# The down product of each expert step moved in front of the next step's up product, in one layer with 64 routed experts

## What is computed

```python
def swiglu(x, wg, wu, wd):
    return (jax.nn.silu(x @ wg) * (x @ wu)) @ wd
...
    idx, wts = route(h2, w_router[i], router_bias[i])
    moe = routed_experts(h2, idx, wts, w_exp_gate[i], w_exp_up[i], w_exp_down[i]) \
        + swiglu(h2, w_sh_gate[i], w_sh_up[i], w_sh_down[i])
    x = x + moe.reshape(B, S, D)
```

## Time and profile before

| | us |
|---|---|
| median of 3 runs | 1059.02 |
| lowest and highest run | 1058.03, 1060.67 |
| profiled execution: span from first to last instruction | 1058.3 |
| of it TensorE matmuls busy | 963.5 |
| VectorE, ScalarE, GpSimd busy | 288.1, 161.2, 168.7 |

### The profile page before, as it was taken

How to read it: one execution, slowest core, us unless ns; L and a number is a source line. 1 busy time by engine, 2 the same in 40 slices (tenths; PEclk the granted TensorE clock), 3 DMA queues, 4 the chain that set the end, 5 groups by cost and what they waited for, 6 DMA issues and landing times.

```text
span 1058.3 us, 15067 instructions
## 1 busy us (share of the span) xinstructions
PE 963.5 (91%) x6147; PEld 433.8 (41%) x6147; DVE 288.1 (27%) x652; ACT 161.2 (15%) x293; POOL 168.7 (16%) x320
## 2 busy tenths in 40 slices
PE   5999999999999899999999999999988887882598
PEld 4554554444444343343333333333323222330487
DVE  3322641002212562344322111111101010110982
ACT  2002230150000101111111111211111111210111
POOL 3235000000001011222222222222221212101100
PEclk9999999999999899999999999999989998996699
DMA  9351211121231818999999999999999999988931
GB/s 334 126 159 42 78 40 53 68 79 40 87 143 36 361 53 325 379 401 407 416 408 413 417 408 405 397 406 373 421 422 421 420 422 421 417 368 306 402 157 40
DMA packets 70692, 292.87 MB, mean 277 GB/s; under 512 B 8204, under 2 KB 30240, under 8 KB 43616
## 3 DMA queue, kind: packets, MB, share of 16 engines
q1 hardware_dynamic: 57872, 255.96, 61.1%
q0 software_dynamic: 12176, 33.86, 8.3%
q10 hardware_dynamic: 576, 2.10, 0.5%
HBM read 275.63 MB, written 25.69 MB: 285 GB/s over the span
## 4 chain that ended last, share of the span: by engine, by line
PE 72%; DMA 22%; DVE 3%; SPq 1%; issue 1%; ACT 1%; POOL 0%; POOLq 0%; DVEq 0%
PE ps L1705 21%; DMA ring<-in_w_exp_up 19%; PE ps L1433 11%; PE ps L1733 8%; PE ps L1813 5%; PE ps L1535 5%; PE ps L1417 3%; PE ps L1377 3%; PE ps L1520 3%; PE ps L1518 3%; PE ps L1354 3%; DMA ring<-accumulator 2%; PE ps L1581 2%; PE ps L1383 1%; PE ps L1566 1%
## 5 line engine op out<-in xcount | busy, mean ns | idle before, releaser
L1705 PE MATMUL ps<-ring,gates 128*32 128x512 f32 x2624 | 298.5, 608 | 34.0 <-DMA ring<-in_w_exp_up 32.5
L1705 PEld LDWEIGHTS ps<-ring,gates 128*32 128x32 f32 x2624 | 91.4, 112 | 235.1 <-issue 233.3
L1733 PE MATMUL ps<-ring,poolbuf 128*32 128x512 f32 x1312 | 149.3, 595 | 1.7 <-ACT actT L768 0.9
L1204 DVE COPY poolbuf<-ps 128x256 f32<-128x256 f32 x41 | 17.4, 425 | 412.8 <-PE ps L1716 412.8
L1433 PE MATMUL ps<-actT,ring 128*128 128x512 f32 x256 | 112.3, 595 | 0.0
L597 POOL TENSOR_TENSOR tickets<-cst 128x1 f32<-128x1 f32 x79 | 14.9, 189 | 393.6 <-ACT actT L768 387.9
L1733 PEld LDWEIGHTS ps<-ring,poolbuf 128*32 128x32 f32 x1312 | 38.8, 109 | 88.7 <-issue 87.4
L1433 PEld LDWEIGHTS ps<-actT,ring 128*128 128x128 f32 x256 | 47.9, 190 | 59.6 <-issue 59.5
L768 ACT ACTIVATE actT<-ps,qT 128x1024 f32<-128x1024 f32 x41 | 45.7, 1114 | 149.2 <-PE ps L1733 149.2
L1354 PE MATMUL ps<-cst,rows 128*128 128x128 f32 x392 | 53.1, 281 | 13.0 <-DMA cst<-in_constants 10.2
L558 POOL TENSOR_SCALAR st<-st 128x1 f32<-128x1 f32 (+2 forms) x17 | 7.4, 434 | 337.2 <-ACT rows L730 241.9
(11 more groups left out here) (226 smaller groups left out, 849.4 us busy)
## 6 DMA issues: line engine op xcount, KB each, us to landing
ring<-in_w_exp_gate SPq DMA_DIRECT2D x64, 1024.0 KB
ring<-in_w_exp_up SPq DMA_DIRECT2D x64, 1024.0 KB, 18.6
ring<-in_w_exp_down SPq DMA_DIRECT2D x64, 1024.0 KB, 14.7
ring<-accumulator SPq DMA_DIRECT2D x16, 1024.0 KB, 11.9
ring<-in_w_gate SPq DMA_DIRECT2D x8, 1024.0 KB, 13.1
ring<-in_w_in SPq DMA_DIRECT2D x5, 1024.0 KB
ring<-in_w_out SPq DMA_DIRECT2D x4, 1024.0 KB
ring<-in_w_ple_gate SPq DMA_DIRECT2D x4, 1024.0 KB
```

The source lines that it names most:

```text
L1705: last = mm(bank(2 + k)[part, :], hgT[k][:, q, part], pair_view(EXPERT_SLOT[js[c]])[:, q], start=(q == 0), stop=(q == KD - 1))
L1733: last = mm(bank(6 + half)[part, :], eactT[r % 2][:, q, part], w[:, q, half * 512:(half + 1) * 512], start=(q == 0), stop=(q == 1))
```

## The change

In step r TensorE now does `up(r)`, `rows_T(r + 1)`, `acts_T(r)`, the lists or the shared part, `down(r)`. Before, `acts_T` and `down` of step r - 1 stood in step r. VectorE copies the transposed activation of step r at the end of its part of step r, behind the copy of the next rows. ScalarE weighs step r in step r, but step 0 in step 1, since its weights are there only then. The order of SyncE's loads and of GpSimd's gathers and scatters is not edited. The whole diff:

```diff
--- before.py
+++ after.py
@@ -787,9 +787,10 @@
                     rows_hi(r + 1, (r + 1) % 2)
                 if JOB_AT + 2 * NT <= r < JOB_AT + JOBS:
                     ple_square(r - JOB_AT - 2 * NT)
+                if r == 1:
+                    weigh(0)
                 if r:
-                    weigh(r - 1)
-            weigh(STEPS - 1)
+                    weigh(r)
 
             def o_start(j):
                 all_scattered(act)
@@ -1219,11 +1220,10 @@
                                         gpost[:, half * 512:(half + 1) * 512], ALU.mult).then_inc(ple_copied, 1)
 
             for r in range(STEPS):
-                if r:
-                    act_T(r - 1, (r - 1) % 2)
                 act_rows(r, r % 2)
                 if r + 1 < STEPS:
                     rows_T(r + 1, (r + 1) % 2)
+                act_T(r, r % 2)
                 if 1 <= r < NGROUP:
                     dve.wait_ge(list_ps, r + 1)
                     rows_of(r, found_of(r))
@@ -1237,7 +1237,6 @@
                     base(n)
                 elif 2 * NT <= n < JOBS:
                     ple_gain(n - 2 * NT)
-            act_T(STEPS - 1, (STEPS - 1) % 2)
 
 
             nc.vector.tensor_copy(o_iota, cst[:, C_IOTA:C_IOTA + CAP]).then_inc(o_iota_ready, 1)
@@ -1738,10 +1737,9 @@
             rows_T(0)
             for r in range(STEPS):
                 up(r)
-                if r:
-                    acts_T(r - 1)
                 if r + 1 < STEPS:
                     rows_T(r + 1)
+                acts_T(r)
                 if 1 <= r < NGROUP:
                     lists(r)
                 n = r - JOB_AT
@@ -1749,10 +1747,7 @@
                     shared_down(n)
                 elif 2 * NT <= n < JOBS:
                     ple_proj(n - 2 * NT)
-                if r:
-                    down(r - 1)
-            acts_T(STEPS - 1)
-            down(STEPS - 1)
+                down(r)
 
 
             def o_start(j):
```

## The result

| | before | after |
|---|---|---|
| median of 4 runs on the same chip, us | 1059.85 (1058.03 to 1061.28) | 1120.26 (1118.25 to 1124.62) |
| profiled span, us | 1058.3 | 1118.1 |

The ratio is 1.056 (95%: 1.0528 to 1.0591). The change costs 60 us; I had forecast 50 of them. In the profiled execution the span grew by 59.8 us.

The account below looks back on a forecast made before the run. TensorE and DMA were taken to bound in turn, both busy from 450 to 600 us, DMA full from 850. 7.1 + 37.6 + 4.4 - 4 + 5 = 50.1 us gave 1109 us, range 1087 to 1126.

Parts of the forecast that it names:

- Part 2: Start: step 1's down product newly waits for the weighing of step 0, which needs the list weights; +7.1 us.
- Part 1: Every step: TensorE waits for its own step's activation before the down product; a list step grows from 12.34 to 12.71 us.
- Part 3: Three-step groups: the first down product waits some 3.3 us for a matrix loaded fifth in its burst; +37.6 us.
- Part 6: Clock: waits in three-step groups drop TensorE to 1.2 GHz, at five of eleven, 1.5 us each; +5 us, bounds 0 and +14.
- Part 4: Second half, two-step groups: DMA engines stay full, 17.4 us a batch against 12.8 us of waiting and products; costs nothing.
- Part 5: End: step 39's down product, ahead of step 40's up product, waits for queued matrices, +4.4 us; earlier final weights, -4.
- rival 4: Three-step groups: the clock falls in every group, up and down products slow, +14 instead of +5 us; 1125 us, chance 0.14.
- Rival 1: Three-step groups: the fifth load lands early enough, only a group's own length counts; 1077 us, chance 0.10.
- Rival 2: Faster: earlier down-matrix loads fill the DMA gap at 700 to 725 us, and the end only gains; 1050 us, chance 0.03.
- Rival 3: Whole kernel: no change, the faster case's gain and the start's 7.1 us cancel; 1059 us, chance 0.03.

Follow-up runs that it names:

- the kernel with the fifth load moved: Changed kernel, with the second expert's down matrix in three-step groups loaded ahead of gate and up of the third and fourth experts: 1083.23 us, ratio 1.0207.
- all loads matched: Changed kernel, with all SyncE expert loads in the new order of use, down matrices ahead of the next gate and up matrices: 1073.94 us, ratio 1.0113.
- transposes in front: Changed kernel, with 24 unread transposes on TensorE in front of the down products of steps 1, 3, 6 and so on to 24: 1115.69 us, ratio 1.0531.
- the second half alone: Kernel before, with the new product order in steps 27 to 40 only and the loads as before: 1063.43 us, ratio 1.0028.
- half of the fifth load's bytes: Changed kernel, loading only the first half of the second expert's down matrix in groups 1 to 9: 1112.6 us, ratio 1.0513.
- the new order in the first half only: Kernel before, with the new product order in steps 0 to 26 only and the loads as before: 1121.03 us, ratio 1.0545.
- the end alone changed: Kernel before, with the new order for steps 39 and 40 only, step 39's down matrices loaded ahead of step 40's up matrices: 1059.76 us, ratio 0.9994.

## Why the prediction was right, and where it was off

The sum in four stretches, in profiled spans; the forecast for the groups includes the clock's 5.

| | forecast | measured |
|---|---|---|
| start, up to U(2) (part 2) | +7.1 | +9.4 (427.23 - 417.88) |
| U(2) to U(26) (parts 1, 3, 6) | +42.6 | +49.6 (773.05 - 427.23 = 345.8 for 296.2) |
| U(26) to the end of D(40) (parts 4, 5) | +4.4 | +6.4 (252.4 for 246.0) |
| behind D(40) (part 5) | -4 | -5.6 (92.7 for 98.3) |
| sum | +50.1 | +59.8 |

U(0), in front of the change, starts 0.6 earlier than before (395.55 for 396.13), so the start costs 9.9 counted from there.

**Part 1, right.** Where no load is late, D starts 2.3 us behind its up product, and seven of the eight groups of the kernel with the fifth load moved last 38.2 to 38.6 us; 3 x 12.71 is 38.1. Over U(2) to U(26) the steps' own lengthening is 12.0 us there (308.2 for 296.2), where 8 x 38.1 and the shared product's 1 give 9.8. With all loads matched it is the larger of the two costs left.

**Part 2, right in its wait, short by the clock.** D(1) starts at 420.73 (forecast 421.45) after 3.08 us for the weighing. But it then takes 6.50 us, and I had summed 3.57. With transposes in front, 3.64 and U(2) at 424.0. These 2.9 us more are what the start has over the 7.1, counted from U(0). I had put the clock's loss at the groups only and forgotten that this new wait is as long as theirs.

**Part 3, right.** The start of D(3k) was taken at 18.3 + 0.14 behind the up product's end; measured are 17.0 to 19.6, on average 18.0. To a tenth all but the 19.6 lie between my bounds (17.0 and 19.3). D(3k) waits in every group. What I had cited against it (the Trainium skill, "DMA: Bandwidth & Descriptors", section "Where 436 GB/s comes from": 435 GB/s, by which there would be no wait) the traces don't bear out for a burst like this one. The kernel with the fifth load moved shows that this one load's place is worth 37 us. That is not the +37.6 of my sum, though the numbers are alike: mine held the steps' own lengthening (9.8) and no slow product, the measured one is the wait (23.4) and the slow products (14.4). For the wait alone I had 37.6 - 9.8 = 27.8. The rate between 430 and 750 us is 346 GB/s, not my 380.

**Part 4, right in its price, a little over its own bound.** From the start of U(28) to that of U(38) a group of two steps lasts 34.5 to 35.3 us, 35.0 on average. That is over the 34.7 at which I wanted to call myself wrong. Before, from U(30) on, where its loads set the pace, such a group lasted 34.6 to 34.8. So the sign has come, by some 0.3 us a group. The bound was drawn too close for the claim that it was to test: from U(26) to U(40) the kernel takes 8.7 us more (237.8 for 229.2), just what part 5 has up to that point (5.0 + 0.14 + 3.57), the DMA share from 850 to 900 us is 1.01 (before 1.02), and the second half alone costs 3 us. The wait of D stands once in each group, before D(28), D(30) and so on to D(38), 3.7 to 5.4 us (besides 0.5 and 1.0 before D(33) and D(35)), and not before nearly every D, as I had written.

**Part 5, right in both signs, but D(39) didn't wait as I had it.** The chain at the end of the kernel after:

```profile
1007.31 3.57 PE ps L1732 x32
1010.88 6.99 PE ps L1704 x64
...
1020.01 5.43 PE ps L1732 x32
...
1034.15 14.68 DMA ring<-accumulator
```

D(39), U(40) and D(40) follow one another as I had them, with a slow D(40), 1.8 too long: this is most of the 2.0 us over the forecast. But the 5.0 us for two queued down matrices were not what set D(39). They landed at 1006.2, and D(39) started at 1007.24 with no idle time in front. What it followed was TensorE's own path: D(38), which waited 3.7 us for its matrices and then took 6.57, the up product of step 39, and 3.2 us of transposes and per-layer product. The two paths end within 1.1 us of each other, so that the number of this step came out is partly luck. Behind D(40) it gained 5.6 where I took 4, inside the bounds: 3.6 up to the start of the accumulator's read (8.7 us for 12.3), 3.3 in the read, and 1.3 were lost again behind it.

**Part 6, the term that was mis-sized.** I took the share of slow products from the kernel before, five of eleven, and 1.5 us each: +5. Seven of eight were slow, by 1.3 to 2.9 us: +14.4, as sums of what they took over 3.64. That is what rival 4 said, and of its 14 us it was nearly exact, though it had U slow as well, and no U was. The rule behind that rival (the Trainium skill, "TensorE: Matmul & The Clock Gate", section "HAM oscillation — how this bites in real kernels": the wait for data at every tile re-throttles the engine at every tile) agrees with seven of eight. I should have weighed it more: in the kernel before, the slow products all lay where DMA hid them, and their rate there said little about a wait of another length. Yet rival 4's sum was too simple as well, and so was my own: both add the slow product to the group's length in full. The run with the transposes took 11.4 us of slow products away and got 4.3 back. The sum of part 3 and part 6 is near the measured one (-0.4 x 8 = -3.2 for the earlier landing, +14.4 for the slow products, less the 5 that I had taken: 6.2 of the 7.0 us missing), but this is bookkeeping along TensorE's path. It is not what each cause is worth if removed: a slow D and the wait in front of it are exchanged for one another through the loads.

**Rival 1** (the loads hide it) came true only when the order of the loads was mended: its 1077 stands beside 1083 (the fifth load moved) and 1074 (all matched). Its 15 us for 24 steps don't follow from the 38.1 for 36.9 us beside them, which give 9.6. **Rival 2** needed the down matrices of step 39 ahead of the up matrices of step 40; given just that, with D(39) moved too, the time did not change (0.9994). D(39) was indeed done ahead, but U(40) started 8.5 later with the two matrices ahead of its own. **Rival 3** was not seen.

**What stays open.** What decides whether a given product runs slow I can't say: behind 24 transposes and 2.34 us of wait one did, behind 2.26 another did not; behind waits without transposes D(15) took 6.54 (2.41 us of wait) and D(21) 3.64 (2.72). D(40) of the kernel after was slow with only 0.72 us idle just in front of it, and not in the kernel with all loads matched, with the same 0.72. Why half of the fifth load's bytes brought its landing only 0.6 us forward is open too.

## What to carry to other kernels

Where single-buffered slots are refilled by one queue in a fixed order, that order is part of the product order: change both together, and before blaming the wait, try to move the one load that is read first ahead of the ones read later. Price a new wait on TensorE with the matmuls behind it at the lower clock, unless independent matmuls can stand in the gap; at a place that loads don't bound, such as the start here, that gives its full price back. Where two resources wait for one another, as the product and the loads do here, a time saved on one comes back only in part (here four to five tenths), so measure the worth of a term by removing it, and don't read it from the chain.

## What the runs showed of the chip that I had not expected

- D(1), behind a wait of 3.08 us, took 6.50 us for 3.64, at a granted clock of 0.55, and D(15) took 6.54 behind 2.41 us. With all loads matched D(1) did the same:

```profile
422.72 6.42 PE L1732 MATMUL ps<-ring,poolbuf 128*32 128x512 f32 x32 [3.08 <-ACT actT L768]
```

- 512 KB in place of 1024 KB behind four loads in a queue: D(3k) started only 0.6 us earlier.
- Slow products move about. With all loads matched the D(3k) were all at 3.6 us, but U at the odd steps from 31 to 39 took 8.7 to 8.8 us instead of 7.1, and the clock from 850 to 900 us was 0.95 in that kernel.

- The read of the accumulator took 14.6 to 14.8 us instead of 17.9 in each kernel with D(39) ahead of U(40) whose chain is shown above, and 18.18 in the one with the new order in the first half only. The bytes are the same. The kernel with the end alone changed has 14.59. So the order at the end makes it; that it is the final weights, which pass earlier there, was my guess in part 5 and was not tried by itself.

The chain of the kernel with the new order in the first half only:

```profile
1035.92 18.18 DMA ring<-accumulator
```
